# RWKV layer on one core: the last output gate's dense matmuls set between the steps of the state pass, and the bonus sums moved into the fifth dense block

## What is computed

```
def rwkv7_scan(r, w, k, v, a, b):
    def step(state, inp):
        r_t, w_t, k_t, v_t, a_t, b_t = inp
        sa = jnp.einsum('bhvk,bhk->bhv', state, a_t)
        state = (state * w_t[:, :, None, :] + sa[..., None] * b_t[:, :, None, :]
                 + v_t[..., None] * k_t[:, :, None, :])
        return state, jnp.einsum('bhvk,bhk->bhv', state, r_t)
...
    y = rwkv7_scan(rh, decay, kh, vh, -kk, kk * ah)
    mean = jnp.mean(y, -1, keepdims=True)
    var = jnp.mean(jnp.square(y - mean), -1, keepdims=True)
    y = ((y - mean) * lax.rsqrt(var + RW_LN_EPS)).reshape(B, S, RW_WIDTH) * ln_w + ln_b
    bonus = jnp.sum(rh * kh * r_k_h, -1, keepdims=True) * vh
    out = (y + bonus.reshape(B, S, RW_WIDTH)) * g
...
        gate_a, gate_b, gate_c = jnp.split(jax.nn.sigmoid(gates), N_BRANCH, axis=-1)
```

## Time and profile before

| | |
|---|---|
| median of 3 runs | 3039.59 us (3037.04 to 3041.13) |
| profiled execution, its time | 3041.51 us |
| profiled execution, its span | 3039.6 us |
| TensorE busy | 2895.9 us (95% of the span) |
| VectorE busy | 1389.2 us (46%) |
| ScalarE busy | 715.3 us (24%) |
| GpSimd busy | 715.0 us (24%) |
| mean granted clock of TensorE | 0.982 of full speed |

### The profile page before, as it was taken

How to read it: one execution, slowest core, us unless ns; L and a number is a source line. 1 busy time by engine, 2 the same in 40 slices (tenths; PEclk the granted TensorE clock), 3 DMA queues, 4 the chain that set the end, 5 groups by cost and what they waited for, 6 DMA issues and landing times.

```text
span 3039.6 us, 60978 instructions
## 1 busy us (share of the span) xinstructions
PE 2895.9 (95%) x25747; PEld 2367.8 (78%) x25747; DVE 1389.2 (46%) x1521; ACT 715.3 (24%) x1017; POOL 715.0 (24%) x454
## 2 busy tenths in 40 slices
PE   4999999999999999999999989899899999999998
PEld 4787978788888888776767767677787888888886
DVE  5655454545454554565635555544533222222222
ACT  3212121212122221244445664000212000000001
POOL 0303020212121121222221112333232333333331
PEclk9999999999999999999999999999999999999999
DMA  5202020101111110233321111433411111111111
GB/s 192 72 19 66 10 72 21 54 24 52 30 45 35 40 36 30 86 101 114 106 80 35 42 56 61 133 118 113 139 58 36 49 48 48 48 48 48 48 48 69
DMA packets 212371, 192.69 MB, mean 63 GB/s; under 512 B 21857, under 2 KB 184251, under 8 KB 212155
## 3 DMA queue, kind: packets, MB, share of 16 engines
q1 hardware_dynamic: 204448, 163.02, 17.6%
q10 hardware_dynamic: 7707, 26.34, 2.2%
HBM read 158.91 MB, written 30.41 MB: 62 GB/s over the span
## 4 chain that ended last, share of the span: by engine, by line
PE 91%; DVE 3%; issue 2%; DMA 1%; ACT 1%; SPq 0%; POOL 0%; DVEq 0%; ACTq 0%; POOLq 0%
PE ps L250 66%; PE ps L811 3%; PE ps L825 2%; PE ps L822 2%; PE ps L789 2%; DMA arena<-in_w_ada 1%; PE ps L874 1%; PE ps L906 1%; PE ps L905 1%; PE ps L996 1%; PE ps L1021 1%; PE ps L1009 1%; DVE arena L1675 1%; PE ps L750 1%; PE ps L757 1%
## 5 line engine op out<-in xcount | busy, mean ns | idle before, releaser
L250 PE MATMUL ps<-x_hi,w_hi 128*128 128x512 f32 (+1 forms) x2576 | 842.9, 402 | 44.2 <-issue 27.5
L250 PE MATMUL ps<-x_lo,w_hi 128*128 128x512 f32 (+1 forms) x2576 | 820.7, 393 | 0.0
L250 PE MATMUL ps<-x_hi,w_lo 128*128 128x512 f32 (+1 forms) x2576 | 819.5, 392 | 0.0
L240 POOL CAST w_hi<-w_raw 128x1024 fp32r<-128x1024 f32 (+2 forms) x221 | 213.0, 964 | 2265.1 <-PE ps L250 1603.6
L250 PEld LDWEIGHTS ps<-x_hi,w_hi 128*128 128x128 f32 (+1 forms) x2576 | 479.6, 190 | 184.3 <-issue 76.5
L250 PEld LDWEIGHTS ps<-x_hi,w_lo 128*128 128x128 f32 (+1 forms) x2576 | 486.9, 189 | 106.2
L250 PEld LDWEIGHTS ps<-x_lo,w_hi 128*128 128x128 f32 (+1 forms) x2576 | 487.9, 189 | 102.5
L242 POOL TENSOR_TENSOR w_lo<-w_raw,w_hi 128x1024 fp32r<-128x1024 f32 (+2 forms) x221 | 486.4, 2201 | 17.7
L2006 DVE TENSOR_TENSOR arena<-ps,arena 128x1024 f32<-128x1024 f32 x22 | 26.9, 1225 | 393.8 <-PE ps L250 393.8
L2023 DVE SCALAR_TENSOR_TENSOR arena<-ps,mod,arena 128x1024 f32<-128x1024 f32 x88 | 113.0, 1284 | 130.4 <-PE ps L250 130.4
L1701 DVE COPY_PREDICATED arena<-hid_lo,ps 128x256 f32<-128x256 int32 x144 | 72.1, 500 | 139.8 <-PE ps L822 88.7
(11 more groups left out here) (269 smaller groups left out, 3514.2 us busy)
## 6 DMA issues: line engine op xcount, KB each, us to landing
w_raw<-in_w_in SPq DMA_DIRECT2D x78, 512.0 KB, 4.0
arena<-in_w_ada SPq DMA_DIRECT2D x48, 512.0 KB, 4.7
w_raw<-in_w_ffn_in SPq DMA_DIRECT2D x44, 512.0 KB, 3.8
gates_sig<-arena ACTq DMA_DIRECT2D x24, 512.0 KB, 2.7
arena<-gates_sig SPq DMA_DIRECT2D x24, 512.0 KB, 3.4
w_raw<-in_w_ffn_out SPq DMA_DIRECT2D x22, 512.0 KB, 3.5
arena<-in_x SPq DMA_DIRECT2D x16, 512.0 KB, 6.9
y_a<-arena ACTq DMA_DIRECT2D x10, 512.0 KB, 2.7
```

Of the source, the lines that this page charges most:

```text
L240: nc.gpsimd.tensor_copy(hi, raw).then_inc(s_whi, 1)
L250: ins = nc.tensor.matmul(dst[h], wp, xp[h], start=first and m == 0, stop=last and m == 2)
```

## The change

Block 5 is no longer one piece behind the pass. Its 48 records are numbered 0 to 47 in the order that they had. Numbers 0 to 5 stand one behind each step c = 1 to 6, four (6 to 9) in step 7 ahead of the second batch's first `y_own`, one (10 to 16) behind each step 8 to 14, and 31 (17 to 47) behind step 15. As block 5 writes banks 0 and 1 while the pass runs, the first batch's `qq @ state` moves from bank 1 to bank 3. The bonus sums are moved from behind block 4 to behind its fifth slice of eight. No arithmetic is added or removed.

```diff
+        STATE_BANK = (1, 3)
+        STATE_FILL = [c if c < BATCH - 1 else c + 3 for c in range(CHUNKS - 1)] + [6 * KT]
...
-                dense(pe, Block("rwkv", 4, i))
-                pe.wait_ge(v_kn, upto(i * 2 + 1))
-                pe.wait_ge(v_c, upto(i * VC + PREP.index("rk") + 1))
-                sums(4, headsum, rw["y1"]).then_inc(r_bon, 1)
+
+                def bonus_sums(k):
+
+                    if k == 4:
+                        pe.wait_ge(v_kn, upto(i * 2 + 1))
+                        pe.wait_ge(v_c, upto(i * VC + PREP.index("rk") + 1))
+                        sums(4, headsum, rw["y1"]).then_inc(r_bon, 1)
+                dense(pe, Block("rwkv", 4, i), after=bonus_sums)
...
+                def last_gate(first, last):
+
+
+                    blk = Block("rwkv", 5, i)
+                    if first == 0:
+                        pe.wait_ge(s_wsplit, upto(blk.before + 1))
+                    for r in range(first, last):
+                        k, part, h = r // 6, r % 6 // 2, r % 2
+                        wp = (w_lo if part == 2 else w_hi)[:, blk.slot, k * P:(k + 1) * P]
+                        xp = (x_lo if part == 1 else x_hi)[:, k, h * 512:(h + 1) * 512]
+                        ins = mm(ps[:, 2 * blk.slot + h, :], wp, xp, start=r < 2, stop=r >= 6 * KT - 2)
+                    if last == 6 * KT:
+                        ins.then_inc(s_dense, 1)
...
-                            ins = mm(bank(c // BATCH, 3, hp)[:, c % BATCH, :], qq[hp, c, :], state[hp, :], start=True, stop=True)
+                            ins = mm(bank(c // BATCH, STATE_BANK[c // BATCH], hp)[:, c % BATCH, :], qq[hp, c, :], state[hp, :], start=True, stop=True)
...
+                    fill = STATE_FILL[c - 1:c + 1]
                     if c + 1 == BATCH:
+                        last_gate(*fill)
                         pe.wait_ge(v_qmg, upto(i * 6 + 6))
                         wait_alone(pe)
                     if c + 1 < CHUNKS:
                         y_own(c + 1)
-                dense(pe, Block("rwkv", 5, i))
+                    if c + 1 != BATCH:
+                        last_gate(*fill)
```

More of the change, by code:

```diff
@@ L1716, in _ @@
                         dve.wait_ge(r_s, upto(i * STEPS + c))
-                        v.scalar_tensor_tensor(SS[:, c + 1, :], bank(B, 3)[:, c % BATCH, :], rw["ff"][:, c:c + 1], ffm[:, c, :], ALU.mult, ALU.add).then_inc(v_s, 1)
+                        v.scalar_tensor_tensor(SS[:, c + 1, :], bank(B, STATE_BANK[B])[:, c % BATCH, :], rw["ff"][:, c:c + 1], ffm[:, c, :], ALU.mult, ALU.add).then_inc(v_s, 1)
                 post = [0]
```

## The result

| | before | changed |
|---|---|---|
| median | 3040.28 us (3037.04 to 3041.13, 4 runs) | 3069.61 us (3062.65 to 3074.52, 4 runs) |
| span of the profiled execution | 3039.6 us | 3065.7 us |

The changed kernel takes 1.0097 of the time of before (95% interval 1.0075 to 1.0119), 29 us more. The forecast was 12 us more, with a range that ended at 3063. The sign was right, and the size was off by a factor of more than two. The changed kernel's four times lie 12 us apart, so a difference of one or two us against its median means nothing.

The account below looks back on a forecast made before the run. TensorE's own queue was taken as the bound. Per pair 1.46 us for the gate and 0.13 for the fill, times 8, made 12.7 us on a median of 3039.6: 3052 us, with an 8 in 10 range of 3046 to 3063.

Parts of the forecast that it names:

- What bounds the kernel: Whole kernel: TensorE, busy for 95% of the span; only time taken off or put on its own queue counts.
- The fill's price: Pass steps with one record: 1.04 us instead of 0.80, 0.235 more each, +3.06 us over 13 steps.
- Step 7: Pass step with four records ahead of `y_own`: 1.73 us instead of 0.80, +0.93.
- The pass and block 5 together: Pass +3.06 and +0.93, block 5 behind it -3.86: +0.13 us a pair, 1.0 us over 8 pairs.
- the "issue" stands: TensorE standing eight times inside L860, 3.7 us in all: up to 3.7 us either way, not in the sum.
- The switches of tile size: Around a lone dense record in the pass: 0.11 us going in, 0.09 coming out, 0.43 us held in all.
- The gate: End of block 4: transposes wait uncovered for ScalarE's `gate(1)`, 1.46 us a pair, 11.7 us over 8 pairs.
- the first weight load: Ahead of the transposes behind block 4: another 0.11 us after the gate, within the 1.46 us exposed.
- The norm: Behind the last pass step: L888 can start at 7.40 us, the 31 records end at 7.41; no wait.
- The clock: Rival: the added quiet stretch of 1.46 us a pair lowers the clock; in every pair 12 us, 3064, chance 0.04.
- the prediction's signs of being wrong: In the profile: steps near 0.9, 0.8 or from 1.15; L912 waiting for the norm; clock below 1.00, 96 to 1260 us.

Follow-up runs that it names:

- e2: The kernel before with only the bonus sums moved behind the fifth slice of block 4, block 5 whole behind the pass: 3048.7 us, 1.0038 of before.
- e1: The changed kernel with the bonus sums back behind block 4, the fill of the pass kept: 3057.3 us, 1.0065 of before.
- e5: The changed kernel with only 7 records in the pass, behind steps 8 to 14, and 41 behind step 15: 3053.6 us, 1.0049 of before.
- e8: The changed kernel with only 7 records in the pass (steps 8 to 14) and the bonus sums back behind block 4: 3037.4 us, 0.9995 of before.
- e3: The changed kernel with TensorE's loop over the 8 pairs written out, so no branch at a turn: 3041.7 us, 1.0012 of before.
- e7: The changed kernel with the bonus sums back behind block 4 and TensorE's loop as four turns of two pairs: 3044.9 us, 1.0020 of before.
- e4: The kernel before with TensorE's loop over the 8 pairs written out: 3050.0 us, 1.0043 of before.

## Why the prediction was wrong

**What bounds the kernel.** Right: each part of the account is time on TensorE's own queue.

**The fill's price.** Right: 1.04 us a step, put together from two edges in other places, was measured. A record starts 0.15 us behind the last small matmul and the next small one 0.43 us later, as at the two edges. Step 7 took 1.78 where 1.73 was said. The pass and block 5 together gave -0.24 us a pair where +0.13 was forecast; most of the rest is that the "issue" stands of 0.2 to 0.6 us in five of the old passes did not come back, which the prediction had left out of its sum as up to 3.7 us either way.

**The switches of tile size.** They were paid in full, and no gap swallowed them: all 104 lone records of the changed kernel hold TensorE for 0.43 us, where a record inside a block takes 0.227. The Trainium skill's page "TensorEngine Tiling (Array Packing)", section Key Properties, says that changing the tiling mode drains TensorE. The traces agree in so far as the two switches of such a record cost 0.20 us together; they don't show a drain as such.

**The gate.** Right: 1.46 us a pair forecast, 1.40 + 0.06 measured; 10.1 us (e2) and 12.3 us (the changed kernel against e1) where 11.7 was said. The hundredth is partly luck. The forecast has 0.11 us for the first weight load ahead of the first transpose, but the two start together (158.30 and 158.31). In its place the second transpose comes 0.06 us late, and the sums' new place costs about 0.05.

**The norm.** The step that failed is this one: "They just meet: no wait, and nothing more to be had." There is indeed no wait: L912 starts 7.43 us behind the start of the last row of L898, as forecast (7.40 to 7.41), and nothing in it waits. But the step left nothing to be lost behind the transposes either, and there the loss was: the distance from the first transpose to the next block 0 grew from 1.72 to 3.53 us in the mean, +1.81 in each of seven turns, 12.7 us, and the sum has no term for it. The point to look at was TensorE's queue, not its array. The wait for the norm is an instruction in the queue, and in all eight pairs of the changed kernel the branch starts 0.17 us behind the norm's end, not before it. The prediction asked who waits behind the block and named three engines; the one thing queued behind the wait besides the transposes was the branch. The 4 us by which block 5 outlived the norm looked like free room. By e5 and e8, 1.6 us of it were; the last 2.1 us were the cover of the branch. Priced by the branch's own row of before, 3.67 us in the median, with the whole lead of 2.1 us gone, this would have been +2.1 a turn, 15 us, and the whole sum 3067; the branches of the changed kernel were shorter, 3.32 in the median. The "issue" gap of 0.74 in front of L250 in the trace of before, the visible end of the branch, was in the timeline and was not read.

The Trainium skill has the rule, on its page "Runtime: NRT & Kernel Launch", section Instruction fetch mechanics: a taken branch to code outside of what is loaded makes the engine fetch it before it goes on. The traces agree, with 3.3 to 3.9 us for a branch taken and 83 ns for the one that leaves the loop. That the time belongs to the branch is shown by e3 and e7, which take the branch away. That it is the loading of code is the page's reading, and the packets of instructions, with the branch's end always 1.35 to 1.51 us behind a landing, agree with it.

**The clock.** It was a rival with a chance of 0.04, and at the wrong place: the gate's stand does not lower it (e2), the turn's does, in three of seven turns here, three in e1, one of three in e7 and none in e5, where TensorE is idle for 0.3 to 0.9 us. It made 4.9 us, and of the prediction's signs of being wrong, the clock below 1.00 between 96 and 1260 us is the one that came; none of them looked at the turn. The sum with both is 3052 + 12.7 + 4.9 = 3070, and 3069.6 was measured. That this fits within 1 us is luck: in the profiled executions the same terms come 4 us too high, as the fill and the solve were 3.9 us cheaper than forecast, and the medians lie further apart than those executions.

**What stays open.** Which of the turns is followed by half clock differs from run to run, and the runs don't show what decides it. It is not the length of the stand alone: in the changed kernel the three turns that were followed by it had the shortest idle times (2.39 to 2.42 us), the other four 2.45 to 2.74. Why the packet of code in the pass of e4 starts so late, at a place where the loop kernels stand 0.7 us at most, was not tested, nor why the branch's lead is 2.1 us.

## What to carry to other kernels

When a wait on the last engine's queue is made to coincide with the end of the work ahead of it, ask what is queued behind the wait: in a hardware loop it is the branch, and slack ahead of the wait's user that looks idle may be what hides part of it (here 2.1 us of 3.7). Work laid over another engine's read of PSUM (here sums over a sigmoid) is a cover; move it only when something else of that length takes its place. Waits with the reason "issue" are worth a look at the transfers: a packet of instructions that lands in such a stand, or just before it, speaks for code that came late. And a gap that is filled with matmuls of another tile size gives back only the gap less two switches: here a record of 0.227 us still made its step 0.24 us longer.

## What was not expected of the hardware

- A taken branch on TensorE's queue took 3.3 to 3.9 us from its start to the next instruction, and the queue came to it at most 2.1 us ahead of the array, however early the norm was ready (1.9 us ahead of the branch in the kernel before, 0.3 in e5).
- Writing the loop out does not always pay: it took the branch out of the kernel before and brought eight stands of 0.8 to 2.8 us between starts, seven of them in the pass, and half clock with five of them (+11 us), while with dense records between the small matmuls there were none.
- A stand of about 2.5 us was followed by 3.4 us at 1.2 GHz (once, in e1, 6.8 us) in some turns and not in others; one of 1.2 us never was, in 8 pairs of e2.
- After a taken branch and in the stands of the pass, TensorE went on 1.2 to 1.7 us behind the landing of a 16 KB packet of instructions, not at once.
